# Two copies instead of one of the residual and RMSNorm tiles in an output-projection loop

## The chip, the cores and the metric

One Trainium2 chip, 8 cores, one program on all of them. The time is the device time in microseconds of the slowest core.

## The reference, cut to what matters

The kernel computes one layer of a decoder block for 2 x 8192 tokens of 1024 channels: an attention and a pooling branch, gated and merged, then a channel sub-layer. The part that the change touches is the end of the first sub-layer and the norm in front of the second one:

```
merged = (jax.nn.sigmoid(g_attn) * (attn @ w_branch_attn[l])
          + jax.nn.sigmoid(g_pool) * (pool @ w_branch_pool[l]))
x = x + gate1 * (merged @ w_out[l])

h2 = rms_norm(x, norm2_g[l]) * (1 + scale2) + shift2
u = causal_dwconv(h2 @ w_up[l], conv_w[l], conv_b[l])
```

## The kernel before, in words

Each core owns 2048 tokens, in 16 tiles of 128, and one tile ahead of them (17 tiles in all). The program is a row of stages with a barrier after each: modulation, input projection, attention, output projection (the one that is changed), up-projection with convolution, down-projection. `modrep` in SBUF holds the six modulation vectors, 1024 floats each, in the order shift1, scale1, gate1, shift2, scale2, gate2.

The output-projection stage (lines 802 to 900) goes over five groups of tiles: one of a single tile, then four of four tiles. In each group it first makes the pooling branch tile by tile (lines 843 to 858, PSUM bank 0), then the merged activations `mergedT` in eight pieces (859 to 873, banks 2 to 5, gates loaded from `SGS`), and then runs a loop over the group's tiles (874 to 899). The text gives the steps of that loop letters, with the tile's place in its group behind:

- M: 16 matmuls of `mergedT` with `Wout`, 8 into bank 6 and 8 into bank 7 (lines 877 to 881), on TensorE (PE)
- G: two products with gate1, one for each bank, into the halves of `tmp3` (882), on VectorE (DVE); Ga and Gb are the halves
- A: `x1t = tmp3 + xo` (885), on VectorE; `xo` is the residual input, loaded by line 876, and `x1t` is stored to `X1S` by line 886
- Q: sum of squares of `x1t` into a column of `small3`, the squares themselves into `junk3`, and its root (889, 890), on ScalarE (ACT)
- R: the reciprocal (891); S: `tmp3 = x1t` times it times G2rep (892); H: `h2b = tmp3 + shift2` (893), all on VectorE
- T: eight transposes of `h2b` into bank 0 (894 to 896), on TensorE; C: the copy of bank 0 into `h2T` (897), on ScalarE

`warm(n)` puts in n dummy matmuls of 512 columns into bank 1, whose result nobody reads: 2 per pooling tile, 3 per piece of `mergedT`, 4 after G and 4 after C of each tile. A dummy depends on the operation that stands ahead of it in the program.

The order on each engine's queue isn't that of the program. Within a stage, `schedule` simulates the engines at build time with costs that are written in the kernel, and takes again and again the operation that can start first, out of the next 48 waiting ones of each engine. These lines of it are spoken of below:

```
f += (LAT if (d.eng != e or d.is_dma) else 0.15) + sl
...
if ok and e == 'tensor' and o.mode != pemode[0]:
    ready = max(ready, te + 0.4)
if ok and o.bg:
    ready = max(ready, te) + 0.25
if ok and (best is None or ready < best[0] - 1e-9):
    best = (ready, e, o)
if ok and ready <= te:
    break
```

`te` is the time up to which the engine is taken, `LAT` is 0.35, `bg` marks a dummy, and the `mode` of a transpose differs from that of a matmul. Keys such as `'tmp3'` or `('ps', 0)` (a PSUM bank) carry the dependences; a key with a slot conflicts with the same slot and with the name alone. DMAs that share a semaphore name wait for each other.

Of the kernel before, what the change touches and what calls it, by code (L numbers as in the profile page):

```python
# [7 lines left out]
F32 = mybir.dt.float32  # L8
BF16 = mybir.dt.bfloat16
AF = mybir.ActivationFunctionType  # L10
# [235 lines left out]
def build_nc():  # L246
# [37 lines left out]
    with ExitStack() as st:  # L284
# [29 lines left out]
        def bank(i, n=512, parts=128, off=0):  # L314
            return psum[0:parts, i * 512 + off: i * 512 + off + n]
# [27 lines left out]
        def TR(out, in_, ident, R, W):  # L343
            P.op('tensor', lambda e: e.transpose(out, in_, ident), R, W, dur=(0.42 if in_.dtype == F32 else 0.12),  # L344
                 mode=(rk(in_.shape[0]), rk(fs(in_)), in_.dtype == F32, True))

        def ACT(out, in_, func, R, W, **kw):
            P.op('scalar', lambda e: e.activation(out=out, in_=in_, func=func, **kw), R, W,  # L348
                 dur=edur('scalar', fs(in_)) + (0.1 if 'accum_out' in kw else 0.0))

        def DMA(q, out, in_, R, W, sem):
            nb = fs(out) * out.shape[0] * (4 if out.dtype == F32 else 2)
            P.op(q, lambda e: e.dma_start(out=out, in_=in_), R, W, dma=sem, dur=2.0 + nb / 120000.0)  # L353

        def TT(eng, out, in0, in1, op, R, W):
            P.op(eng, lambda e: e.tensor_tensor(out=out, in0=in0, in1=in1, op=op), R, W, dur=edur(eng, fs(out)))  # L356
# [9 lines left out]
        def STT(out, in0, scalar, in1, op0, op1, R, W):  # L366
            P.op('vector', lambda e: e.scalar_tensor_tensor(out=out, in0=in0, scalar=scalar, in1=in1, op0=op0, op1=op1), R, W,  # L367
                 dur=edur('vector', fs(out)))
# [443 lines left out]
        t1 = T3([512], F32)  # L812
        t2 = T3([512], F32)
        mergedT = T3([8, 512], BF16)
        xo = T3([1024], F32)
        x1t = T3([1024], F32)
        tmp3 = T3([1024], F32)
        h2b = T3([1024], BF16)
        junk3 = T3([1024], BF16)
        small3 = T3([16], F32)  # L820

        CDMA(Wba, wba_d.rearrange("(h d) c -> d h c", d=64), ['Wba'], cast=True)
# [17 lines left out]
        for (tf, ntl) in chunks:  # L840
            N = ntl * 128
            tok0 = tf * 128
            for tl in range(ntl):
                ti = tf + tl
                cb, pb = (0, 4) if ti != 1 else (8, 12)
                for g in range(4):
                    o = bank(0)[:, g * 128:(g + 1) * 128]
                    MM(o, p_own[:, ti, g * 128:(g + 1) * 128], Am[:, cb + g, :], True, ti == 0, ['p_own', 'Am'], [('ps', 0)])
                    if ti >= 1:
                        MM(o, p_own[:, ti - 1, g * 128:(g + 1) * 128], Am[:, pb + g, :], False, True, ['p_own', 'Am'], [('ps', 0)])  # L850
                CP('scalar', pooledT, bank(0).rearrange("p (g t) -> p g t", t=128), [('ps', 0)], ['pooledT'])
                for g in range(4):
                    MM(bank(0)[:, g * 128:(g + 1) * 128], poolw[:, g, :], pooledT[:, g, :], True, True,
                       ['poolw', 'pooledT'], [('ps', 0)])
                for g in range(4):
                    ACT(pool2T[:, g, tl * 128:(tl + 1) * 128], bank(0)[:, g * 128:(g + 1) * 128], AF.Copy,
                        [('ps', 0), 'pscale'], [('pool2T', tl)], scale=pscale[:, g:g + 1])
                warm(2)
            for mt in range(8):
                si = mt % 2  # L860
                DMA('sync', sgc[si][:, 0, 0:N], SGS[mt, :, tok0:tok0 + N], (), [('sgc', si)], 'sgc%d' % si)
                DMA('sync', sgc[si][:, 1, 0:N], SGS[8 + mt, :, tok0:tok0 + N], (), [('sgc', si)], 'sgc%d' % si)
                ba, bp = 2 + (mt % 2), 4 + (mt % 2)
                for hh in range(8):
                    MM(bank(ba, N), Wba[0:64, hh, mt * 128:(mt + 1) * 128], attnT[0:64, hh, tok0:tok0 + N],
                       hh == 0, hh == 7, ['Wba', 'attnT'], [('ps', ba)])
                for g in range(4):
                    MM(bank(bp, N), Wbp[:, g, mt * 128:(mt + 1) * 128], pool2T[:, g, 0:N], g == 0, g == 3,
                       ['Wbp', 'pool2T'], [('ps', bp)])
                TT('vector', t1[:, 0:N], bank(ba, N), sgc[si][:, 0, 0:N], ALU.mult, [('ps', ba), ('sgc', si)], ['t1'])  # L870
                TT('vector', t2[:, 0:N], bank(bp, N), sgc[si][:, 1, 0:N], ALU.mult, [('ps', bp), ('sgc', si)], ['t2'])
                TT('vector', mergedT[:, mt, 0:N], t1[:, 0:N], t2[:, 0:N], ALU.add, ['t1', 't2'], [('mergedT', mt)])
                warm(3)
            for tl in range(ntl):
                ti = tf + tl
                DMA('sync', xo, xw_v[47 + ti], (), ['xo'], 'xo')
                for half in range(2):
                    wb = 6 + half
                    for k in range(8):
                        MM(bank(wb), mergedT[:, k, tl * 128:(tl + 1) * 128], Wout[:, k, half * 512:(half + 1) * 512],  # L880
                           k == 0, k == 7, ['mergedT', 'Wout'], [('ps', wb)])
                    TT('vector', tmp3[:, half * 512:(half + 1) * 512], bank(wb), gate1rep[:, half * 512:(half + 1) * 512],
                       ALU.mult, [('ps', wb), ('modrep', 2)], [('tmp3', half)])
                warm(4)
                TT('vector', x1t, tmp3, xo, ALU.add, ['tmp3', 'xo'], ['x1t'])
                DMA('sync', X1S[ti], x1t, ['x1t'], [('X1S', ti)], 'x1s')
                sm = small3[:, (ti % 4) * 4:(ti % 4) * 4 + 4]
                smk = ('small3', ti % 4)
                ACT(junk3, x1t, AF.Square, ['x1t'], ['junk3', smk], accum_out=sm[:, 0:1])
                ACT(sm[:, 1:2], sm[:, 0:1], AF.Sqrt, [smk], [smk], scale=1.0 / 1024.0, bias=epsb)  # L890
                RECIP(sm[:, 2:3], sm[:, 1:2], [smk], [smk])
                STT(tmp3, x1t, sm[:, 2:3], G2rep, ALU.mult, ALU.mult, ['x1t', smk, 'G2rep'], ['tmp3'])
                TT('vector', h2b, tmp3, shift2rep, ALU.add, ['tmp3', ('modrep', 3)], ['h2b'])
                for k in range(8):
                    TR(bank16(0)[:, k * 128:(k + 1) * 128], h2b[:, k * 128:(k + 1) * 128], ident_bf,
                       ['h2b', 'ident_bf'], [('ps', 0)])
                CP('scalar', h2T[:, :, ti * 128:(ti + 1) * 128], bank16(0).rearrange("p (k t) -> p k t", t=128),
                   [('ps', 0)], [('h2T', ti)])
                warm(4)
# [170 lines left out]
```

How the kernel before makes its waits and increments, by code:

```python
            def body(e):  # L198
# [9 lines left out]
                        if k not in need or need[k][1] < d.val:  # L208
                            need[k] = (d.sem, d.val)
                    if o.force is not None:
                        d = o.force
                        k = id(d.sem)
                        if k not in need or need[k][1] < d.val:
                            need[k] = (d.sem, d.val)
                    for k, (sem, val) in need.items():
                        if wt.get(k, 0) >= val:
                            continue
                        e.wait_ge(sem, val)
                        wt[k] = val
                    ins = o.fn(e)
                    if o.is_dma:
                        ins.then_inc(o.sem, 16)
                    elif o.flag:
                        ins.then_inc(o.sem, 1)
                if eng_name in ('sync', 'gpsimd') or final:
                    for sem, val in dma_final:
                        k = id(sem)
                        if wt.get(k, 0) >= val:
                            continue
                        e.wait_ge(sem, val)
                        wt[k] = val
```

## Time and profile before

| | us |
|---|---|
| median of 2 runs | 3096.95 (3095.92 to 3097.97) |
| the profiled execution | 3089.25 |
| span of its slowest core (core 5) | 3087.7 |
| spans of its eight cores | 3065.0 to 3087.7 |
| output-projection stage on core 5 | from 2136.6 to 2554.5 |

The span runs from the first to the last instruction of the core that was profiled. Times in rows are microseconds from the start of that span unless they are marked ns. Helpers issue all operations, so the lines in rows are those of helpers: L340 a matmul, L344 a transpose, L348 and L372 ScalarE's activations and copies, L353 a DMA, L356 a VectorE operation on two tensors, L367 the one with a scalar column (S), L380 the reciprocal.

### The profile page before, as it was taken

The page shows a single profiled execution, that of the slowest core. Times are in us where ns is not written, and L with a number is a line of the kernel's source. Part 1 is how long each engine was busy: PE and PEld are TensorE (multiplying, and loading weights), DVE is VectorE, ACT ScalarE, POOL GpSimd, SP SyncE. Part 2 cuts the span into 40 slices and gives each one's busy share as a digit, 9 for nine tenths or more (in the row PEclk, how much of TensorE's full clock was granted, in tenths as well). Part 3 has the DMA queues.
Part 4 walks back from the last instruction along what each step waited for, and adds up shares of the span by engine and source line. Part 5 has one row for each costly group of instructions (what it writes and reads, how often), then busy time and mean ns, then how long its engine had stood idle before and what let it go on. Part 6 is the DMA issues. An engine that isn't in the chain of part 4 may idle for free. (4 is left out here: it accounts for less than half of the span.)

```text
span 3087.7 us, 43503 instructions; the slowest of 8 cores (3065.0 to 3087.7 us)
## 1 busy us (share of the span) xinstructions
PE 2446.0 (79%) x15542; PEld 1361.1 (44%) x15542; DVE 1145.2 (37%) x1507; ACT 1659.6 (54%) x2148; POOL 55.7 (2%) x63
## 2 busy tenths in 40 slices
PE   6668888996587878788787878786777778999499
PEld 2234434442455555465555545554333333444144
DVE  0257663221323232322323232321244445888322
ACT  0157775543486868687686868685122115777300
POOL 0000000000000000000000000000000001111000
PEclk9789999998798989899898989898689888999799
DMA  8774442213301010100001000003222213333532
GB/s 264 196 166 136 137 125 82 76 56 104 84 1 32 1 32 1 32 1 19 14 1 32 1 18 1 1 1 56 54 72 80 82 64 41 38 39 37 93 102 103
DMA packets 132450, 191.29 MB, mean 62 GB/s; under 512 B 57168, under 2 KB 102608, under 8 KB 128336
## 3 DMA queue, kind: packets, MB, share of 16 engines
q1 hardware_dynamic: 76192, 158.48, 16.7%
q0 software_dynamic: 56048, 30.02, 7.9%
q8 instruction: 130, 2.13, 0.3%
q14 instruction: 80, 0.66, 0.1%
HBM read 173.24 MB, written 45.22 MB: 71 GB/s over the span
## 5 line engine op out<-in xcount | busy, mean ns | idle before, releaser
L340 PE MATMUL psum<-arena 128*128 128x512 bf16 (+8 forms) x14434 | 2356.8, 313 | 454.8 <-ACT arena L348 116.5
L340 PEld LDWEIGHTS psum<-arena 128*128 128x128 bf16 (+3 forms) x14434 | 1288.4, 102 | 1505.8 <-issue 919.8
L348 ACT ACTIVATE arena<-psum 128x1024 bf16<-128x1024 f32 (+3 forms) x1113 | 999.6, 911 | 407.7 <-PE psum L340 373.1
L356 DVE TENSOR_TENSOR arena<-psum,arena 128x256 f32<-128x256 f32 (+4 forms) x535 | 276.6, 527 | 1238.5 <-PE psum L340 1130.5
L348 ACT ACTIVATE arena<-arena 128x1024 bf16<-128x1024 f32 (+4 forms) x383 | 336.5, 889 | 326.3 <-DVE arena L356 221.2
L367 DVE SCALAR_TENSOR_TENSOR arena<-arena 128x2048 f32<-128x2048 f32 (+3 forms) x195 | 331.7, 1701 | 91.3 <-ACT arena L348 78.4
L356 DVE TENSOR_TENSOR arena<-arena 128x1024 bf16<-128x1024 f32 (+5 forms) x208 | 236.9, 1139 | 70.4 <-PE psum L344 46.1
L372 ACT COPY arena<-psum 128x512 f32<-128x512 f32 (+1 forms) x258 | 185.0, 719 | 137.2 <-PE psum L344 67.6
L344 PE MATMUL psum<-arena 128*128 128x128 bf16 (+1 forms) x1108 | 89.2, 234 | 180.5 <-DVE arena L356 141.8
L380 DVE RECIPROCAL arena<-arena 128x1 f32<-128x1 f32 (+3 forms) x234 | 146.4, 633 | 124.1 <-ACT arena L348 116.4
L344 PEld LDWEIGHTS psum<-arena 128*128 128x128 bf16 (+1 forms) x1108 | 72.7, 111 | 213.9 <-issue 213.9
L372 ACT CAST arena<-psum 128x512 bf16<-128x512 f32 x98 | 57.1, 583 | 105.3 <-PE psum L340 105.3
L523 DVE TENSOR_REDUCE arena<-arena 128x8 f32<-128x512 f32 x81 | 55.4, 684 | 156.1 <-ACT arena L348 156.0
L348 ACT ACTIVATE arena<-psum,arena 128x512 bf16<-128x512 bf16 (+2 forms) x193 | 89.7, 474 | 39.6 <-PE psum L340 26.5
L348 ACT ACT_TABLE_LOAD x19 | 24.4, 1283 | 157.4 <-DMA arena<-xw 80.4
L356 DVE TENSOR_TENSOR arena<-arena,psum 64x256 bf16<-64x256 f32 (+2 forms) x73 | 28.9, 395 | 91.6 <-PE psum L340 91.3
L377 DVE MEMSET arena<- 128x1632 bf16 (+3 forms) x11 | 11.5, 1048 | 137.3 <-PE psum L340 97.2
L353 POOL DMA_DIRECT2D arena<-wup x44 | 38.5, 875 | 680.5 <-POOLq L234 415.0
L374 DVE COPY arena<-psum 128x256 f32<-128x256 f32 (+2 forms) x96 | 42.2, 439 | 22.9 <-PE psum L344 15.9
L353 POOL DMA_DIRECT2D arena<-wba x1 | 0.7, 685 | 1371.7 <-POOLq L234 1371.7
L377 POOL MEMSET arena<- 128x4096 bf16 (+1 forms) x3 | 7.2, 2409 | 611.4 <-POOLq L234 611.1
L686 DVE TENSOR_REDUCE arena<-arena 128x17 f32<-128x544 f32 x24 | 17.2, 717 | 1.8
(18 smaller groups left out, 45.9 us busy)
## 6 DMA issues: line engine op xcount, KB each, us to landing
arena<-xw SPq DMA_DIRECT2D x81, 512.0 KB, 4.3
arena<-ada_w SPq DMA_DIRECT2D x16, 1536.0 KB, 8.2
arena<-wup POOLq DMA_DIRECT2D x44, 256.0 KB, 4.6
X1S<-arena SPq DMA_DIRECT2D x17, 512.0 KB, 2.9
VS<-arena SPq DMA_DIRECT2D x16, 512.0 KB, 3.5
KS<-arena SPq DMA_DIRECT2D x16, 512.0 KB, 3.5
SGS<-arena SPq DMA_DIRECT2D x8, 1024.0 KB, 4.5
arena<-KS SPq DMA_DIRECT2D x8, 1024.0 KB, 8.4
```

The source lines that it names most:

```text
L340: P.op('tensor', lambda e: e.matmul(out, lhsT=lhsT, rhs=rhs, start=start, stop=stop), R, W, dur=d, mode=(rk(lhsT.shape[0]), rk(fs(lhsT)), ...
L344: P.op('tensor', lambda e: e.transpose(out, in_, ident), R, W, dur=(0.42 if in_.dtype == F32 else 0.12), mode=(rk(in_.shape[0]), rk(fs(in_ ...
L348: P.op('scalar', lambda e: e.activation(out=out, in_=in_, func=func, **kw), R, W, dur=edur('scalar', fs(in_)) + (0.1 if 'accum_out' in kw ...
L353: P.op(q, lambda e: e.dma_start(out=out, in_=in_), R, W, dma=sem, dur=2.0 + nb / 120000.0)
L356: P.op(eng, lambda e: e.tensor_tensor(out=out, in0=in0, in1=in1, op=op), R, W, dur=edur(eng, fs(out)))
L367: P.op('vector', lambda e: e.scalar_tensor_tensor(out=out, in0=in0, scalar=scalar, in1=in1, op0=op0, op1=op1), R, W, dur=edur('vector', fs ...
L372: P.op('scalar', lambda e: e.copy(out, in_), R, W, dur=edur(eng, fs(out)))
L374: P.op(eng, lambda e: e.tensor_copy(out, in_), R, W, dur=edur(eng, fs(out)))
L377: P.op(eng, lambda e: e.memset(ap, val), (), W, dur=edur(eng, fs(ap)))
L380: P.op('vector', lambda e: e.reciprocal(out, in_), R, W, dur=0.08 + 8 * fs(out) / 900.0)
L523: P.op('vector', lambda e: e.tensor_reduce(out=sm, in_=sq.rearrange("p (h d) -> p h d", d=64), axis=AX.X, op=ALU.add), ['sq'], [smk])
L686: P.op('vector', lambda e: e.tensor_reduce(out=m, in_=src, axis=AX.X, op=ALU.max), SCK, ['gm'], dur=0.15 + nt * 32 / 900.0)
```

## The change

The five tiles `xo`, `x1t`, `tmp3`, `h2b` and `junk3` become lists of two; the tile number's parity picks one. The second copies lie in memory that is free by then: shift1, scale1 and scale2 in `modrep`, and G1rep behind it (elements 12288 onward of the bf16 view). The keys get the index as a slot or as part of the name, and the two DMAs get two semaphores each. PSUM banks, the dummies, `small3` and the order in which the program lists the operations stay.

```diff
-        xo = T3([1024], F32)
-        x1t = T3([1024], F32)
-        tmp3 = T3([1024], F32)
-        h2b = T3([1024], BF16)
-        junk3 = T3([1024], BF16)
+        xo = [T3([1024], F32), modrep[:, 4096:5120]]
+        x1t = [T3([1024], F32), modrep[:, 0:1024]]
+        tmp3 = [T3([1024], F32), modrep[:, 1024:2048]]
+        h2b = [T3([1024], BF16), a16[:, 12288:12288 + 1024]]
+        junk3 = [T3([1024], BF16), a16[:, 12288 + 1024:12288 + 2048]]
...
-                DMA('sync', xo, xw_v[47 + ti], (), ['xo'], 'xo')
+                bi = ti % 2
+                DMA('sync', xo[bi], xw_v[47 + ti], (), [('xo', bi)], 'xo%d' % bi)
...
-                    TT('vector', tmp3[:, half * 512:(half + 1) * 512], bank(wb), gate1rep[:, half * 512:(half + 1) * 512],
-                       ALU.mult, [('ps', wb), ('modrep', 2)], [('tmp3', half)])
+                    TT('vector', tmp3[bi][:, half * 512:(half + 1) * 512], bank(wb), gate1rep[:, half * 512:(half + 1) * 512],
+                       ALU.mult, [('ps', wb), ('modrep', 2)], [('tmp3_%d' % bi, half)])
                 warm(4)
-                TT('vector', x1t, tmp3, xo, ALU.add, ['tmp3', 'xo'], ['x1t'])
-                DMA('sync', X1S[ti], x1t, ['x1t'], [('X1S', ti)], 'x1s')
+                TT('vector', x1t[bi], tmp3[bi], xo[bi], ALU.add, ['tmp3_%d' % bi, ('xo', bi)], [('x1t', bi)])
+                DMA('sync', X1S[ti], x1t[bi], [('x1t', bi)], [('X1S', ti)], 'x1s%d' % bi)
...
-                ACT(junk3, x1t, AF.Square, ['x1t'], ['junk3', smk], accum_out=sm[:, 0:1])
+                ACT(junk3[bi], x1t[bi], AF.Square, [('x1t', bi)], [('junk3', bi), smk], accum_out=sm[:, 0:1])
...
-                STT(tmp3, x1t, sm[:, 2:3], G2rep, ALU.mult, ALU.mult, ['x1t', smk, 'G2rep'], ['tmp3'])
-                TT('vector', h2b, tmp3, shift2rep, ALU.add, ['tmp3', ('modrep', 3)], ['h2b'])
+                STT(tmp3[bi], x1t[bi], sm[:, 2:3], G2rep, ALU.mult, ALU.mult, [('x1t', bi), smk, 'G2rep'], ['tmp3_%d' % bi])
+                TT('vector', h2b[bi], tmp3[bi], shift2rep, ALU.add, ['tmp3_%d' % bi, ('modrep', 3)], [('h2b', bi)])
                 for k in range(8):
-                    TR(bank16(0)[:, k * 128:(k + 1) * 128], h2b[:, k * 128:(k + 1) * 128], ident_bf,
-                       ['h2b', 'ident_bf'], [('ps', 0)])
+                    TR(bank16(0)[:, k * 128:(k + 1) * 128], h2b[bi][:, k * 128:(k + 1) * 128], ident_bf,
+                       [('h2b', bi), 'ident_bf'], [('ps', 0)])
```

## Rows read from the trace of the kernel before

**Rows 1.** Busy time by engine, clock, DMA share: the stage, then its four tile loops

```profile
2136.60:2554.50 417.90, 296.79 (x1378) 123.10 (x1378) 159.37 (x222) 77.97 (x154) 2.87 (x4) 0.83 0.27 76
2253.36:2290.84 37.48, 27.36 (x127) 11.40 (x128) 20.75 (x25) 9.82 (x16) 0.00 (x0) 0.91 0.36 123
2338.00:2376.70 38.70, 27.01 (x128) 11.25 (x127) 21.80 (x26) 9.82 (x16) 0.00 (x0) 0.91 0.35 120
2424.90:2465.20 40.30, 28.76 (x127) 11.71 (x127) 20.78 (x25) 9.82 (x16) 0.00 (x0) 0.88 0.34 114
2513.50:2553.13 39.63, 30.34 (x128) 12.19 (x129) 20.81 (x25) 9.82 (x16) 0.00 (x0) 0.84 0.27 93
```

**Rows 2.** Timeline of VectorE in the first four-tile loop: start, duration, operation, [idle before]

```profile
2258.62 1.29 DVE L356 TENSOR_TENSOR arena<-psum,arena 128x512 f32<-128x512 f32 x2 [5.26 <-PE psum L340]
2260.16 1.23 DVE L356 TENSOR_TENSOR arena<-arena 128x1024 f32<-128x1024 f32 x1 [0.24 <-DVE arena L356]
2263.11 0.16 DVE L380 RECIPROCAL arena<-arena 128x1 f32<-128x1 f32 x1 [1.73 <-ACT arena L348]
2263.39 1.29 DVE L367 SCALAR_TENSOR_TENSOR arena<-arena 128x1024 f32<-128x1024 f32 x1
2264.78 1.23 DVE L356 TENSOR_TENSOR arena<-arena 128x1024 bf16<-128x1024 f32 x1
2266.11 1.29 DVE L356 TENSOR_TENSOR arena<-psum,arena 128x512 f32<-128x512 f32 x2
2267.64 1.23 DVE L356 TENSOR_TENSOR arena<-arena 128x1024 f32<-128x1024 f32 x1 [0.24 <-DVE arena L356]
...
2287.40 1.23 DVE L356 TENSOR_TENSOR arena<-arena 128x1024 bf16<-128x1024 f32 x1 [0.17 <-DVE arena L367]
```

**Rows 3.** Timeline of ScalarE, same loop: root of Q1, then C1 and C4

```profile
2262.72 0.29 ACT L348 ACTIVATE arena<-arena 128x1 f32<-128x1 f32 x1
2266.96 1.01 ACT L372 COPY arena<-psum 128x1024 bf16<-128x1024 bf16 x1 [3.95 <-PE psum L344]
...
2289.58 1.01 ACT L372 COPY arena<-psum 128x1024 bf16<-128x1024 bf16 x1 [4.00 <-PE psum L344]
```

**Rows 4.** Timeline of TensorE: the first loop, a slow transpose ahead of it, slow projection matmuls

```profile
2194.88 1.01 PE L344 MATMUL psum<-arena 128*128 128x128 bf16 x8 [5.11 <-DVE arena L356]
...
2259.46 4.86 PE L340 MATMUL psum<-arena 128*128 128x512 bf16 x21 [0.30 <-DVE arena L356]
2266.26 0.61 PE L344 MATMUL psum<-arena 128*128 128x128 bf16 x8 [1.94 <-DVE arena L356]
2267.05 6.39 PE L340 MATMUL psum<-arena 128*128 128x512 bf16 x21 [0.18 <-PE psum L344]
...
2288.88 0.61 PE L344 MATMUL psum<-arena 128*128 128x128 bf16 x8 [3.17 <-DVE arena L356]
2290.84 2.79 PE L340 MATMUL psum<-arena 128*128 128x128 bf16 x15 [1.35 <-ACT arena L372]
...
2513.71 6.52 PE L340 MATMUL psum<-arena 128*128 128x512 bf16 x16 [1.27 <-DVE arena L356]
```

**Rows 5.** Timeline of VectorE: first G of the other loops, one H that waits

```profile
2344.19 1.29 DVE L356 TENSOR_TENSOR arena<-psum,arena 128x512 f32<-128x512 f32 x2 [5.04 <-PE psum L340]
...
2431.43 1.29 DVE L356 TENSOR_TENSOR arena<-psum,arena 128x512 f32<-128x512 f32 x2 [6.51 <-PE psum L340]
...
2454.26 1.23 DVE L356 TENSOR_TENSOR arena<-arena 128x1024 bf16<-128x1024 f32 x1 [1.59 <-PE psum L344]
...
2520.12 1.29 DVE L356 TENSOR_TENSOR arena<-psum,arena 128x512 f32<-128x512 f32 x2 [6.56 <-PE psum L340]
```

**Rows 6.** Loads of xw (KB, us to landing); a wait and the busy times near the stage's start

```profile
arena<-xw SPq DMA_DIRECT2D x81, 512.0 KB, 4.3
...
2168.77 1.01 PE L340 MATMUL psum<-arena 128*128 128x512 bf16 x2 [3.29 <-DMA arena<-wout]
...
2140.00:2186.00 46.00, 20.09 (x136) 11.56 (x137) 6.53 (x24) 3.34 (x6) 0.05 (x1) 0.62 0.70 125
```

## The prediction

> **What bounds the kernel now.** I began with the span in equal stretches. The output-projection stage is 417.9 us of the 3087.7 us span, and in it no engine is full: TensorE is busy for 296.8 us, VectorE for 159.4 us, ScalarE for 78.0 us, and the DMA engines have a share of 0.27 [rows 1]. So the stage runs on waits, and averages say nothing about what the change is worth. The change touches only the tile loop at the end of each group of four tiles. I cut that loop out of the timeline for each group, from the first gate product G1 to the first matmul behind the last copy C4 (in the last group, to the dummies that close the stage): 2258.62 to 2290.84 is 32.2 us, 2344.19 to 2376.70 is 32.5, 2431.43 to 2465.20 is 33.8 and 2520.12 to 2553.13 is 33.0 [rows 2, 5]; the ends are those of the windows, set at that matmul [rows 1]. Together 131.5 us, about 4% of the kernel; nothing that happens there can give more than a part of it.
>
> Next, the VectorE timeline of one section [rows 2]. The reader is to see a period: G1 starts at 2258.62 and G2 at 2266.11, 7.5 us later, and the next tiles repeat it. Inside: G 1.29, A 1.23 after a gap of 0.24, then 1.73 us of idling that ScalarE's square and root end, R 0.16, S 1.29, H 1.23. That is 5.2 us of work and some 2.3 us of gaps. G2 can't start before H1 has read `tmp3`, so VectorE has nothing to put into the 1.73 us. A 16-matmul group M2 is meanwhile done early: it starts 0.84 us after G1, and with its five dummies takes 4.86 us [rows 4]. VectorE's one-tile chain bounds the section, then its tail H4, T4, C4: 2287.40 + 1.23 to 2290.84 is 2.2 us [rows 2 to 4]. In the third group H waits 1.59 us for transposes, because there is one `h2b` [rows 5].
>
> **What the change takes away.** No arithmetic is added or removed. With two copies of every tile, G2 need not wait for H1, and the 1.73 us can be filled with G2. The waits for the load of `xo` and the store of `x1t` are relaxed too, which I cost at nothing: the median `xw` load lands 4.3 us after its issue [rows 6], and between the end of A1 (2260.16 + 1.23), which frees the buffer, and A2 at 2267.64 lie 6.3 us [rows 2]; without that cover it would cost up to the 4.3 us per tile.
>
> The Trainium skill, page "Trainium Kernel Development and Optimization", section "Best Practices", advises double-buffering so that DMA and compute overlap. By that alone one would expect the loads to be the gain; the row above says they were covered, and no term of the sum rests on this sentence.
>
> **The new order, from the scheduler.** The queues are written in the order that the kernel's own list scheduler picks, so I walked its rule through the section, with the costs in the code, for the order only. Three of its rules decide. On the PE queue a plain matmul whose inputs are there goes before a dummy (dummies are charged 0.25), and a dummy goes before a transpose (a change of mode is charged 0.4). Among ready operations the earliest wins, ties by program order. Once banks 6 and 7 are freed early, M3 and M4 are always ready before, or within the 0.4 of, T1. So I get, on PE: M1 M2 M3 M4 with two or three dummies in between, then about 12 dummies, the last four of which wait for G4, and only then T1, T2, about 8 dummies, T3, T4. On VectorE: G1 A1 G2a R1 G2b S1 A2 H1 G3 R2 A3 S2 H2 R3 G4a S3 G4b A4 R4 S4 H3 H4. H3 lands behind S4 since it rewrites the `h2b` that T1 reads. On ScalarE: the four squares and roots, then C1 C2 C3 C4. In the kernel before, C1 ran at 2266.96 between the squares of tiles 1 and 2 [rows 3]; transposes and copies, which were spread over the section, now gather at its end. All share bank 0, so they can't overlap each other.
>
> **The sum for one section**, zero at the start of G1, with 0.11 us between VectorE instructions. G1 and A1 end at 2.76. G2a needs 14 of M2's 16 matmuls (the halves alternate), each 4.86/21 = 0.231 us: 0.84 + 14 x 0.231 + 0.1 = 4.2. Then 0.69 for G2a (half of a pair, a little over 1.29/2), R1 to 5.2, G2b to 6.0, S1 to 7.4, A2 to 8.7, H1 to 10.0, G3 to 11.4, R2, A3 to 13.0, S2 to 14.4, H2 to 15.8, R3, G4a to 16.8, S3 to 18.2, G4b to 19.0, A4 to 20.5. R4 waits 1.73 again, to 22.2, S4 ends at 23.8, H3 at 25.1, H4 at 26.5 [rows 2, 4]. In the kernel before, H4 ended 30.0 us after G1. VectorE alone thus gains 3.5 us a section.
>
> The tail takes most of this back. PE's last four dummies start at 19.3. With the clock at its upper level (transposes 0.61 us for eight, dummies 0.23 each), T1 ends at 20.8, ScalarE is through Q4 1.62 us after A4 (2261.39 to 2263.01, that is A1's end to the end of the root), at 22.1, C1 takes 1.01 to 23.2, T2 starts 0.25 later (C4's end at 2290.59 to the matmul at 2290.84) and ends at 24.1, C2, 0.09 behind it, ends at 25.2, the 8 dummies at 26.3, T3 at 27.0, C3 at 28.1, T4 at 29.0, C4 at 30.1, and the next matmul starts at 30.35 [rows 2 to 4]. At the lower level, where eight transposes took 1.01 us and sixteen projection matmuls 6.52, 0.41 each [rows 4], the dummies take 3.3 us and the same steps end at 32.7. The trace before does not show which it would be: behind the 1.94 us gap ahead of T1 matmuls got slower (M3 and its dummies took 6.39 us where the same 21 took 4.86 as M2), while T4, after a wait of 3.17 us, took the short 0.61 [rows 4]. Neither is nearer, so I take the middle, 31.5. Four sections: 126.0 against 131.5, a gain of 5.5 us; the ends are 121.4 (a gain of 10.1) and 130.8 (a gain of 0.7).
>
> The page "PSUM — Partial Sum Buffer", section "Engine vs sequencer instructions", of the Trainium skill says that the queues of ScalarE and VectorE are strictly first in, first out. It is why C1 stands behind Q4; the ScalarE rows agree as far as they go, and the sum used only the rows.
>
> **What is added.** Tile 1's `xo` has its own buffer, so its 512 KB are now asked for at the stage's start, where PE waits 3.29 us for `wout` while data moves at 125 GB/s [rows 6]. If it pushes all of these back it costs 0.52 MB / 125 GB/s = 4.2 us; if it falls into slack, nothing, and a gain has no reason. TensorE is busy 20.1 of those 46 us, so part of the stretch waits for something, but only 3.29 us of it for that weight; I take 1.0, near the lower end. In the SP queue the load stands ahead of the second `SGS` loads, which wait for the first ones anyway. What waits behind T1 on PE, the out-projection, has gone before it; behind C1 on ScalarE stand only copies. The first tile, alone in its group, keeps its order.
>
> Sum: -5.5 + 1.0 = -4.5 us against the profiled execution (3089.25, of which 3087.7 is the span; the four sections are 131.5 of it). The two runs shown have a median of 3096.95, 7.7 us over the profiled one, so I set the same difference against it: 3092.5, given as 3092.
>
> **Rivals.** (1) VectorE stays the bound and the transposes find room earlier, for instance if T1 and T2 come before the dummies. Then a section ends at H4 26.5 + 2.2 = 28.7, four give 114.8, a gain of 16.7 less 1.0: 3081. For it: idle PE time in the section. Against: the scheduler's charges above.
>
> (2) Slower. TensorE's clock falls in the sections, since PE now has waits ahead of M3, M4 and the last dummies. The section then takes its 32.7, and one of M2 to M4 at the lower level delays its G by 14 x (0.41 - 0.231) = 2.5 us: 35.2 a section, 140.8 for four, 9.3 more than before, with the load 10.3: 3107. For it: M3's row in the kernel before, 6.39 us for the same 21 matmuls that took 4.86 as M2 [rows 4]. Against: dummies fill the gaps, and the sections' granted clock was 0.84 to 0.91 [rows 1]. It decides from the point at which that mean falls below about 0.75.
>
> The Trainium skill's page "TensorE: Matmul & The Clock Gate", section "A second HAM failure mode: psum-queue depth-cycling", describes just that, short idles between matmul groups that cycle banks making the clock swing; no row here shows it caused by bank cycling.
>
> (3) The change does nothing that can be seen: G2 is early but the tail eats all, or G2 keeps waiting for another shared thing (banks, `small3`). 3097.
>
> **How the numbers follow.** The forecast has 0.55, rival 1 0.18, rival 2 0.15, rival 3 0.12. The forecast's bounds with the load's bounds run from 3087 (10.1 gained) to 3100 (0.7 gained, 4.2 lost). The range takes in most of rivals 1 and 2 and their neighbours: 3080 to 3105. A measurement of this kernel can tell about 2% (62 us) from no change. To be 2% faster, the four sections would have to lose half of their 131.5 us, where VectorE's own work is already 4 x 20.8 = 83 us; to be 2% slower, each would have to grow by 15 us, more than the 64 projection matmuls add at the lower level (64 x 0.18 = 11.5). I give 0.02 to faster, 0.02 to slower, 0.96 to the same.
>
> **What would show it.** In the changed kernel: on VectorE the 1.73 us wait ahead of R stays whole only for tile 4, and behind A1 some 1.4 us of it stands ahead of G2a; A4 ends near 20.5 after G1; H3 and H4 stand together near 25; T1 comes after the last matmuls and a long row of dummies; four copies C1 to C4 stand in a row at the end of each section, each behind its transposes; a section lasts 30 to 33 us. I am wrong if T1 comes between M2 and M4, if a section lasts under 29 us, if its granted clock is under 0.75, or if the first section's start moves by more than 4 us.

## The result, and the profile after

| | before | after |
|---|---|---|
| median of the runs that are compared, us | 3096.95 | about 3081 |
| profiled execution (span of its slowest core), us | 3089.25 (3087.7) | 3079.12 (3077.6) |
| ratio of the times, 95% interval | | 0.9946 (0.993 to 0.9962) |
| output-projection stage, mean of 8 cores (lowest to highest), us | 418.1 (411.1 to 426.0) | 406.6 (400.6 to 408.0) |

The ratio is a gain of 0.0054 x 3096.95 = 16.7 us (12 to 22), where 4.5 us had been forecast. Runs in which one half of the chip ran at a lower clock stand outside the ratio. The stage accounts for 11.5 us of it in the profiled executions; the up-projection (336.6 and 336.9 us) and the down-projection (193.3 and 194.5) behind it did not shorten. What the timed runs have beyond that may lie in the longest stage of any core, which went from 426.0 to 408.0; that is argued, not shown.

First, the busy times of the changed kernel in the stage and its four loops, on its slowest core (core 7), with the columns of [rows 1].

```profile
2138.41:2545.95 407.54, 290.41 (x1378) 121.37 (x1378) 156.04 (x222) 77.11 (x154) 2.87 (x4) 0.84 0.28 78
2259.57:2297.57 38.00, 27.69 (x121) 11.39 (x122) 19.93 (x24) 9.61 (x16) 0.00 (x0) 0.84 0.38 121
2342.91:2379.60 36.69, 26.74 (x121) 11.15 (x122) 19.93 (x25) 9.61 (x16) 0.00 (x0) 0.86 0.40 126
2425.62:2461.79 36.17, 26.22 (x121) 11.01 (x122) 19.92 (x25) 9.61 (x16) 0.00 (x0) 0.86 0.39 128
2507.16:2543.62 36.46, 27.02 (x125) 11.48 (x126) 19.93 (x24) 9.61 (x16) 0.00 (x0) 0.86 0.24 87
```

The four windows went from 37.5, 38.7, 40.3 and 39.6 us [rows 1] to 38.0, 36.7, 36.2 and 36.5. The M matmuls ahead of G1 are in them, as before.

Then VectorE in the first loop, beside [rows 2].

```profile
2265.75 1.29 DVE L356 TENSOR_TENSOR arena<-psum,arena 128x512 f32<-128x512 f32 x2 [6.18 <-PE psum L340]
2267.21 1.23 DVE L356 TENSOR_TENSOR arena<-arena 128x1024 f32<-128x1024 f32 x1 [0.17 <-DVE arena L356]
2270.04 0.69 DVE L356 TENSOR_TENSOR arena<-psum,arena 128x512 f32<-128x512 f32 x1 [1.60 <-PE psum L340]
2270.65 0.15 DVE L380 RECIPROCAL arena<-arena 128x1 f32<-128x1 f32 x1
...
2283.44 2.36 DVE L356 TENSOR_TENSOR arena<-arena 128x1024 f32<-128x1024 f32 x2 [0.24 <-DVE arena L356]
2287.10 0.16 DVE L380 RECIPROCAL arena<-arena 128x1 f32<-128x1 f32 x1 [1.30 <-ACT arena L348]
2287.37 1.28 DVE L367 SCALAR_TENSOR_TENSOR arena<-arena 128x1024 f32<-128x1024 f32 x1
2288.83 1.23 DVE L356 TENSOR_TENSOR arena<-arena 128x1024 bf16<-128x1024 f32 x1 [0.17 <-DVE arena L367]
```

G2a stands between A1 and R1, and waits 1.60 us for M2's first bank; R1 no longer waits. The row of two at 2283.44 is A4 and H3. Only R4 still waits for ScalarE. H4 ends at 2290.06, 24.3 us after G1 (30.0 before).

TensorE and ScalarE in the same loop, beside [rows 4] and [rows 3].

```profile
2266.59 3.99 PE L340 MATMUL psum<-arena 128*128 128x512 bf16 x17 [0.30 <-DVE arena L356]
2270.88 4.06 PE L340 MATMUL psum<-arena 128*128 128x512 bf16 x18 [0.30 <-DVE arena L380]
2276.16 4.04 PE L340 MATMUL psum<-arena 128*128 128x512 bf16 x18 [1.23 <-DVE arena L356]
2280.36 0.61 PE L344 MATMUL psum<-arena 128*128 128x128 bf16 x8
2286.95 1.01 PE L344 MATMUL psum<-arena 128*128 128x128 bf16 x8 [5.99 <-ACT arena L372]
2288.11 5.60 PE L340 MATMUL psum<-arena 128*128 128x512 bf16 x16
2293.86 0.61 PE L344 MATMUL psum<-arena 128*128 128x128 bf16 x8
2295.72 0.61 PE L344 MATMUL psum<-arena 128*128 128x128 bf16 x8 [1.25 <-ACT arena L372]
...
2297.57 1.04 PE L340 MATMUL psum<-arena 128*128 128x128 bf16 x10 [0.51 <-ACT arena L372]
```

```profile
2284.76 1.06 ACT L348 ACTIVATE arena<-arena 128x1024 bf16<-128x1024 f32 x1 [5.05 <-DVE arena L356]
2285.72 0.19 ACT L348 ACTIVATION_READ_ACCUMULATOR arena<-arena 128x1 f32 x1
2285.81 0.99 ACT L372 COPY arena<-psum 128x1024 bf16<-128x1024 bf16 x1
...
2288.05 1.01 ACT L372 COPY arena<-psum 128x1024 bf16<-128x1024 bf16 x1 [1.05 <-PE psum L344]
2294.56 1.01 ACT L372 COPY arena<-psum 128x1024 bf16<-128x1024 bf16 x1 [5.50 <-PE psum L344]
2296.41 1.01 ACT L372 COPY arena<-psum 128x1024 bf16<-128x1024 bf16 x1 [0.84 <-PE psum L344]
```

The reader sees M2, M3 and M4 in a row with five dummies, then T1 and the tail: T1 is done at 2280.97, but its copy C1 stands in ScalarE's queue behind the square of tile 4 and starts at 2285.81, so T2 waits 5.99 us; 16 dummies of 5.60 us follow, and T3, whose `h2b` was ready at 2285.80, starts only at 2293.86. From G1 to the next matmul are 31.8 us (32.2 in [rows 2, 4]).

To see where the rest came from I cut the whole stage of every core into the same four parts per group: *pool* (from the last copy of the group before to the last cast of a pooled tile), *merge* (to the last sum that makes `mergedT`), *M* (to G1), *loop* (to the end of C4). The first group has one tile. Means of eight cores, us:

```
             one tile               group 2              group 3              group 4              group 5
before  6.3 41.1  4.1  9.7   18.1 34.6  5.4 32.1  17.1 32.1  5.4 32.5  17.3 32.5  5.9 32.7  17.2 32.6  6.1 32.8
after   6.3 43.5  4.1  9.7   21.5 35.3  5.7 31.4  14.8 30.8  5.3 31.1  14.8 32.0  5.1 31.0  14.8 30.8  5.2 31.0
```

Added up over groups 2 to 5: loop -5.5, M -1.4, merge -3.0, pool -3.8, and +2.4 in the one tile's merge part: -11.3 of the stage's -11.5. In groups 3 to 5 alone the pool parts lost 7.2 us. The busy times show how. In the kernel before (core 5), first the pool part of group 2, then pool and merge of group 3:

```profile
2197.00:2220.19 23.19, 20.36 (x78) 8.34 (x78) 0.69 (x1) 6.75 (x16) 0.00 (x0) 0.50 0.00 0
...
2290.59:2307.10 16.51, 12.64 (x78) 5.83 (x78) 0.69 (x1) 6.75 (x17) 0.00 (x0) 0.90 0.00 1
2307.10:2339.16 32.06, 25.04 (x99) 9.29 (x99) 15.48 (x23) 1.47 (x4) 0.00 (x0) 0.89 0.19 54
```

and in the changed kernel (core 7):

```profile
2297.43:2312.17 14.74, 10.64 (x76) 5.06 (x76) 0.69 (x1) 6.75 (x16) 0.00 (x0) 1.00 0.00 0
2312.17:2342.91 30.74, 24.52 (x107) 9.30 (x107) 15.48 (x23) 1.47 (x5) 0.00 (x0) 1.00 0.20 57
```

The pool part runs 76 instead of 78 matmuls in 10.64 us instead of 12.64; the granted clock is 1.00 instead of 0.90, and merge runs 107 matmuls, eight more, in less time. A pool part of the old order has two more values. One is 23.2 us, with the clock at its lower level (0.50, 1.2 of 2.4 GHz) from end to end. Of the 24 pool parts of groups 3 to 5 (8 cores) three were near that (22.8 to 23.2 us) before and none after; of the 8 of group 2 it was two before and six after. The other is 15.5 us, in three of the 24, with the clock near its upper level; here on core 7, group 3:

```profile
2285.84:2301.32 15.48, 11.35 (x78) 5.24 (x78) 0.69 (x1) 6.75 (x16) 0.00 (x0) 0.98 0.00 1
```

So at nearly the same clock the new order is worth 0.7 us a pool part (15.5 to 14.8). By that estimate the order has some 2 of the 7.2 us, and the clock the other 5; it was 1.00 in all 24 of these parts after the change.

### The profile page after: what moved, and what is told of

Its sections match the earlier page's. It is cut to its first block and busy times, and to the rows that moved or that the text cites. A ratio compares the mean times of both kernels' runs of the same rounds, so it can differ in the third digit from the quotient of the medians.

```text
span 3077.6 us, 43493 instructions; the slowest of 8 cores (3062.9 to 3077.6 us)
## 1 busy us (share of the span) xinstructions
PE 2440.0 (79%) x15542; PEld 1359.5 (44%) x15542; DVE 1142.1 (37%) x1507; ACT 1657.8 (54%) x2148; POOL 55.7 (2%) x63
## 5 line engine op out<-in xcount | busy, mean ns | idle before, releaser
L340 PE MATMUL psum<-arena 128*128 128x512 bf16 (+9 forms) x14434 | 2349.3, 313 | 447.3 <-ACT arena L348 111.4
L348 ACT ACTIVATE arena<-psum 128x1024 bf16<-128x1024 f32 (+3 forms) x1113 | 998.9, 911 | 411.1 <-PE psum L340 376.7
L348 ACT ACTIVATE arena<-psum,arena 128x512 bf16<-128x512 bf16 (+2 forms) x193 | 89.7, 474 | 40.3 <-PE psum L340 27.2
L377 DVE MEMSET arena<- 128x1632 bf16 (+3 forms) x11 | 11.5, 1048 | 137.5 <-PE psum L340 97.1
L374 DVE COPY arena<-psum 128x256 f32<-128x256 f32 (+2 forms) x96 | 42.2, 439 | 22.9 <-PE psum L344 15.9
```

Of the source, the lines that this page charges most:

```text
L340: P.op('tensor', lambda e: e.matmul(out, lhsT=lhsT, rhs=rhs, start=start, stop=stop), R, W, dur=d, mode=(rk(lhsT.shape[0]), rk(fs(lhsT)), ...
L374: P.op(eng, lambda e: e.tensor_copy(out, in_), R, W, dur=edur(eng, fs(out)))
L377: P.op(eng, lambda e: e.memset(ap, val), (), W, dur=edur(eng, fs(ap)))
```

## The experiments

Ratios are to the kernel before, from timed runs on the same chip; stage and parts are means of eight cores of one profiled execution. The two profiled stages of the changed kernel are 406.6 and 407.4, but the cores of one execution differ by up to 15 us (411.1 to 426.0 before), so a stage of a single profile says less than the ratio.

**The changed kernel again.** No edit.

> The changed kernel itself, once more, as the yardstick for the others on the same chip. On the cores of its first profile the stage took 406.6 us on average (before: 418.1), made up of four tile loops of 31.0 to 31.4 us (before 32.1 to 32.8), pooling parts of groups 3 to 5 of 14.8 us (before mostly 16.5), their merge parts of 30.8 to 32.0 (before 32.1 to 32.6), a merge part of the lone first tile of 43.5 us (before 41.1), and a pooling part of the second group of 16.4 us on two cores and 23.2 us on six (before 16.4 on six, 23.2 on two). All theories expect the same again within 2 us per part, and a ratio to the kernel before of 0.993 to 0.997.

Ratio 0.9938 (0.9917 to 0.9959), stage 407.4, loops 31.5, 31.1, 30.9 and 31.0, pool 23.2 in group 2 and 14.8 behind it (clock 1.00 in all 24). The pattern repeats; 23.2 in group 2 now on all eight cores.

**The buffers without the new order.** Two copies and all semaphores as changed, but each engine's queue in the order of the kernel before, since the scheduler goes by the old dependences (`sdeps` are those of single tiles):

```diff
...
-                    for d in o.deps:
+                    for d in o.sdeps:
...
```

> The changed kernel with all its second buffers, keys and semaphores, but every engine's queue in the order of the kernel before (the scheduler is shown the old single-buffer dependences). Theory A, the gain comes from the new order of the queues, which the buffers only permit: tile loops stay near 32.2 us each, losing at most the one wait of H3 for transposes, the pooling parts stay at 16.5 and the merge parts at 32, the lone tile's merge part stays at 41; stage 416 to 419 us, ratio 0.998 to 1.001. Theory B, the buffers themselves take away waits at run time: tile loops of about 31 us and a stage near 411 us, ratio 0.998 or less. Theory C, a denser tile loop keeps TensorE's clock up for the parts behind it: since the loop is as before, no gain here either, ratio 1.

Ratio 1.0007 (0.998 to 1.0034), stage 421.5, loops 127.4 together (130.1 before), pool 21.5, 16.2, 18.6 and 18.1, merge 131.8. The buffers alone take 2.7 us off the loops and nothing off the kernel. What pays is the order that the scheduler makes of them. Of the 24 pool parts of groups 3 to 5 the nine at a clock of 0.99 or 1.00 took 15.5 us again, five at 0.50 took 23.2.

**The order behind the loop without the buffers.** The kernel before, with twelve dummies instead of four behind the last copy of a group:

```diff
-                warm(4)
+                warm(12 if tl == 3 else 4)
```

> The kernel before, with single buffers, and eight more dummy matmuls after the last tile of each group of four. The scheduler then puts these dummies into the gaps of the next group's pooling part, and the branch matmuls, which it had put there, come behind the third and fourth pooling tile, nearly as in the changed kernel. Theory A: pooling parts of groups 3 to 5 fall from 16.5 to about 14.8 us and their merge parts from 32 to about 31, 8 us in all, tile loops unchanged at 32 to 33, 2 us more at the stage's end; stage about 412 us, ratio 0.997 to 0.999. Theory C, the shorter parts come from a steadier clock behind denser tile loops: parts stay at 16.5 and 32, the eight dummies cost 2 us more at the end; stage near 420, ratio 1.000 to 1.001.

Ratio 0.9972 (0.9953 to 0.9991): about half of the gain with single tiles. Loops 129.6, pool 15.5, 15.9 and 15.7 in groups 3 to 5, merge 31.2, 30.7 and 31.8. Group 5's pool and merge on its slowest core (core 5):

```profile
2463.11:2478.64 15.53, 12.37 (x78) 5.51 (x78) 0.69 (x1) 6.77 (x17) 0.00 (x0) 0.89 0.00 1
2478.64:2509.30 30.66, 24.52 (x107) 9.30 (x107) 15.48 (x23) 1.48 (x4) 0.00 (x0) 0.99 0.18 52
```

The merge part has the 107 matmuls and nearly the time (30.66 us) of the changed kernel: behind the loop the eight dummies bring the changed kernel's order, but for the place of two dummies. The merge parts of groups 3 to 5 take 93.7 us together, 93.6 in the changed kernel and 97.2 before.

**No dummies in the loop.** The changed kernel without its two `warm(4)` lines in the tile loop:

```diff
                     TT('vector', tmp3[bi][:, half * 512:(half + 1) * 512], ...
-                warm(4)
...
                    [('ps', 0)], [('h2T', ti)])
-                warm(4)
```

> The changed kernel without the eight dummies per tile in the tile loop (136 of 204 in the stage). T1 then goes ahead of M4 and T2 to T4 follow without dummies between them, and the next group's branch matmuls move back into the gaps of its pooling part, as in the kernel before. Theory A, order decides: loops of 27 to 29 us in place of 31, pooling parts back at 16.5 and merge parts back at 32, stage about 405, ratio 0.993 to 0.996. Theory C, the dummies keep TensorE's clock up: without them the clock falls to its lower level, pooling parts take the 23.2 us that were seen at that level and loops 33 or more, stage over 425, ratio over 1.002.

Ratio 0.9977 (0.9937 to 1.0018), stage 415.9. The loops fall to 27.2, 26.8, 26.8 and 27.3, 16.4 us less than in the changed kernel, and every pool part of every core is 22.3 us. The slowest core (core 5), loop, pool and merge:

```profile
2265.80:2293.03 27.23, 14.76 (x84) 6.64 (x82) 19.92 (x24) 9.73 (x16) 0.00 (x0) 0.86 0.46 155
2293.03:2315.37 22.34, 18.68 (x74) 7.91 (x74) 0.69 (x1) 6.77 (x16) 0.00 (x0) 0.50 0.00 0
2315.37:2347.67 32.30, 25.21 (x100) 9.31 (x99) 15.47 (x23) 1.48 (x4) 0.00 (x0) 0.87 0.19 53
```

74 matmuls take 18.68 us at 0.50, where the changed kernel's 76 take 10.64 at 1.00. The place of the branch matmuls isn't the reason: they stand in the pooling's gaps as in the kernel before, and there, with 16 dummies ahead of T4, 21 of the 24 pool parts of groups 3 to 5 ran at 0.88 or more. So it is the dummies left out here (136 of the stage's 290; the 204 above is a miscount) that had kept the clock up, as far as this run shows. The loops came as theory A has them, the pool parts as theory C. The page "TensorE: Matmul & The Clock Gate", section "HAM oscillation — how this bites in real kernels", of the Trainium skill says that a TensorE that waits for DMA between bursts drops to the lower clock, and advises a loop that keeps it busy; this run agrees as to the clock, with 0.50 for 1.00, though its waits are for ScalarE and VectorE.

**Fewer dummies between T2 and T4.** In the changed kernel's TensorE queue, of the 16 dummies between T2 and T3 four stay, six go behind T3 and six behind T4 (`w` are the dummies, `t` the transposes):

```diff
...
+            w, t = pe[i + 1:i + 17], pe[i + 17:i + 33]
+            pe[i + 1:i + 33] = w[:4] + t[:8] + w[4:10] + t[8:] + w[10:]
...
```

> The changed kernel with one thing moved on TensorE's queue and nothing else: of the sixteen dummies that stand between T2 and T3 of a four-tile loop, four stay, T3 follows, then six, T4, and the last six. The order of everything behind the loop stays as it is, which the run with cheaper transposes could not hold. Theory A, the loop's tail is made by those dummies: T3 at about 23.5 us after G1, T4 at 25 to 26, loops of 27 to 28 us in place of 31.1, the last six dummies under the wait for C4; parts behind unchanged (14.8 and 30.8); stage 391 to 396, ratio 0.988 to 0.991. Rival, what the cheaper transposes gained in the loop is necessarily lost behind it, since the dummies have to run somewhere: loops of 28, pooling parts or merge parts 3 us longer, stage 405, ratio 0.994.

Ratio 0.9973 (0.9945 to 1.0002), stage 414.6. The loops are 2 us shorter each (116.3 together); pool 21.5, 18.0, 15.4 and 16.7 and merge 33.8, 33.7, 35.4 and 33.2 take it back and more. The queue behind the moved dummies is the same, and no dummy is added or left out. Pool and merge of group 3 on the slowest core (core 5):

```profile
2283.05:2301.94 18.89, 15.15 (x81) 6.45 (x78) 0.69 (x1) 6.78 (x16) 0.00 (x0) 0.78 0.00 1
2301.94:2336.06 34.12, 28.60 (x108) 10.26 (x107) 15.48 (x23) 1.48 (x4) 0.00 (x0) 0.85 0.18 50
```

108 matmuls in 28.60 us at 0.85, where 107 take 24.52 at 1.00. So it is not only the order behind the loop: the clock there changed when nothing but twelve dummies had moved. Nor is it how close they stand, since eight dummies now stand right ahead of the pooling, and two in the changed kernel. Of the 24 pool parts of groups 3 to 5, nine ran at 0.78 or 0.79 (18.8 to 19.0 us) and fifteen at 1.00 (15.4 us); which stretch of dummies decides isn't shown.

**Two copies of `tmp3` and `h2b` alone.** `xo`, `x1t` and `junk3` single again:

```diff
-                DMA('sync', xo[bi], xw_v[47 + ti], (), [('xo', bi)], 'xo%d' % bi)
+                DMA('sync', xo[0], xw_v[47 + ti], (), [('xo', 0)], 'xo0')
...
-                DMA('sync', X1S[ti], x1t[bi], [('x1t', bi)], [('X1S', ti)], 'x1s%d' % bi)
+                DMA('sync', X1S[ti], x1t[0], [('x1t', 0)], [('X1S', ti)], 'x1s0')
```

> The changed kernel with two copies of tmp3 and h2b only; xo, x1t and junk3 are single as before. Theory A, the loads and stores were covered and what counts is that G need not wait for H: the queue order of the parts behind the loop is the new one, so they keep 14.8 and 31 us; A2 may wait for the single xo (issue half a microsecond after A1, 4.3 us to landing), so loops of 31 to 33 us; stage 406 to 412, ratio 0.994 to 0.997. Rival: the second copies of xo and x1t are what pays, and without them the gain goes: loops of 33 us or more, ratio 0.998 to 1.

Ratio 0.995 (0.9923 to 0.9978), stage 402.4, loops 122.4 (124.6 in the changed kernel). No loss: the loads and stores were covered, as the prediction had it. The Trainium skill's page "Trainium Kernel Development and Optimization", section "Best Practices", advises the second buffer for them; here it gave nothing that can be measured.

**The early load held back.** Tile 1's load of `xo` waits for the first tile's `x1t`:

```diff
-                DMA('sync', xo[bi], xw_v[47 + ti], (), [('xo', bi)], 'xo%d' % bi)
+                DMA('sync', xo[bi], xw_v[47 + ti], [('x1t', 0)] if ti == 1 else (), [('xo', bi)], 'xo%d' % bi)
```

> The changed kernel, but the load of the residual input of tile 1 waits for the sum of tile 0, as in the kernel before, instead of being issued at the stage's start beside the weights. If the early load is what lengthened the lone tile's merge part, that part goes back from 43.5 to about 41 us, and the stage from 406.6 to about 404; if it also set off the long pooling part of the second group (23.2 us on six cores of eight), that part falls to 16.5 on most cores and the stage goes to about 400; ratio 0.991 to 0.995. If the longer first part is scatter, nothing moves: ratio as the changed kernel.

Ratio 0.993 (0.9908 to 0.9952), stage 404.3; the one tile's merge part is 41.5 us (43.5 and 42.4 in the two profiles of the changed kernel, 41.1 before). The early load costs 1 to 2 us there. Group 2's pool stays at 22.3, so the load is not what makes it slow.

**Transposes made cheap to the scheduler.** The charge for a change of mode, 0.4, becomes 0.1 ahead of a transpose:

```diff
-                        ready = max(ready, te + 0.4)
+                        ready = max(ready, te + (0.4 if not o.mode[3] else 0.1))
```

> The changed kernel, but the scheduler charges transposes 0.1 in place of 0.4 for the change of mode, so that they go before the dummies: T1 comes before M4, T2 after it, T3 two dummies later, and eight dummies stand between T3 and T4 in place of sixteen between T2 and T3. Theory A, the tail of the tile loop is made by dummies that stand ahead of T3 on TensorE's queue (5.6 us of them in the changed kernel's first loop, while H3 had been done for 8 us): loops of about 28 us in place of 31.1; the parts behind them, of which the order changes only a little, stay within 1 us; stage about 395 us, ratio 0.990 to 0.992. Rival: the tail is VectorE's own chain up to H4, and the order of the transposes changes nothing: loops of 31 us, ratio as the changed kernel, 0.994.

Ratio 0.9933 (0.9909 to 0.9956), stage 414.1. The loops fall to 110.4 together, 27.6 each: rival 1's section, without its gain. The merge parts of groups 3 to 5 are 39.6, 40.5 and 40.5 us, at a mean clock of 0.79: the scheduler filled them in another order, with the branch matmuls that used to stand in the pooling's gaps. The ratio and the profiled stage don't fit here (20 us against 4); I draw nothing from it but that the loop's gain didn't come through: the ratio is the changed kernel's.

**A second bank for the transposes.** The changed kernel, T of even tiles in bank 4:

```diff
+                tb = 0 if bi else 4
...
-                CP('scalar', h2T[:, :, ti * 128:(ti + 1) * 128], bank16(0).rearrange("p (k t) -> p k t", t=128),
-                   [('ps', 0)], [('h2T', ti)])
+                CP('scalar', h2T[:, :, ti * 128:(ti + 1) * 128], bank16(tb).rearrange("p (k t) -> p k t", t=128),
+                   [('ps', tb)], [('h2T', ti)])
```

> The changed kernel, with the transposes of even tiles in PSUM bank 4, which is idle in the tile loop, in place of bank 0, so that copies and transposes of neighbouring tiles need not wait for each other, and the next group's pooling, which works in bank 0, need not wait for C4. The scheduler then puts most of the next group's pooling ahead of T4. Theory A: the chain through the shared bank 0 costs real time; the pooling parts of groups 3 to 5 (14.8 us each behind the loop) move largely into the loop's tail, stage 380 to 395 us, ratio 0.983 to 0.990. Rival: ScalarE and TensorE then collide (pooling copies ahead of C4), and what is gained in one part is lost in the other: stage 400 to 410, ratio 0.992 to 0.996.

Ratio 0.9918 (0.9889 to 0.9948), stage 397.1. Bank 0 is now free for the next group's pooling before the section ends, so the loops (39.8 us in groups 2 to 4) contain it, and the pool parts are below zero (-1.2 and three times -3.3). The merge parts grow to 41 to 42, since the branch matmuls no longer have the pooling's gaps. In groups 3 to 5 that is no gain: loop and next pooling together fall by 28.3 us against the changed kernel, and merge grows by 31.8. The gain is at the lone first tile, whose loop and group 2's pooling fall from 31.2 to 11.4 us, while merge grows by 5.7.

**Both: second bank and late load.** The edits of the two runs together.

> The changed kernel with the transposes of even tiles in PSUM bank 4, and tile 1's load of xo held back until the first tile's x1t is there. If the two gains add, the stage means 395 to 396 us (397.1 with two banks alone, less the 1 to 2 us that the late load gave), the lone tile's merge part 41 to 41.5 us, and the ratio to the kernel before 0.990 to 0.992. If the late load's gain was chance of the profile, the stage stays at 397 and the merge part at 43.

Ratio 0.9882 (0.9843 to 0.9921), stage 392.2 (389.7 to 396.5): the lowest ratio of all, though its interval overlaps that of the second bank without the late load; 3053.4 us (median of four) against 3088.0 (of six) for the kernel before. The one tile's merge part is 40.5 (43.0 with two banks alone). TensorE at the end of group 3's section, slowest core (core 0):

```profile
2334.49 1.00 PE L344 MATMUL psum<-arena 128*128 128x128 bf16 x15 [0.18 <-DVE arena L380]
2340.69 1.01 PE L344 MATMUL psum<-arena 128*128 128x128 bf16 x8 [5.20 <-ACT arena L372]
2341.85 3.52 PE L340 MATMUL psum<-arena 128*128 128x512 bf16 x16
...
2347.36 1.04 PE L340 MATMUL psum<-arena 128*128 128x128 bf16 x10 [0.47 <-ACT arena L348]
2348.78 1.25 PE L340 MATMUL psum<-arena 128*128 128x128 bf16 x8 [0.39 <-ACT arena L372]
...
2357.35 0.61 PE L344 MATMUL psum<-arena 128*128 128x128 bf16 x8
```

T1 and T2 go together (the row of 15; one of the 16 isn't in the trace), T3 follows, and the pooling (the rows of 10 and 8) runs ahead of T4 at 2357.35, which waits for nothing.

**The second bank alone.** The kernel before, single tiles, T of even tiles in bank 4.

> The kernel before (single tiles), only with the transposes of even tiles in PSUM bank 4. Theory 'order': what pays is that the next group's pooling matmuls find room inside the section once bank 0 is free for them, and no second copy of a tile is needed for that: stage 400 to 408 us, ratio 0.992 to 0.996, parts of loop and next pooling together 45 to 47 us (49.8 before). Theory 'copies': VectorE's one-tile chain still ends the section, so nothing moves: stage 414 to 422, ratio 0.999 to 1.002, loop and next pooling 49 to 50 us.

Ratio 0.9905 (0.9874 to 0.9936), stage 398.4. Loop and next pooling together are 40.1, 41.7 and 40.4 us where they were 49.2, 49.8 and 49.9; merge takes back part of it (41.1, 41.0, 34.7, 41.1). The lone tile's loop and group 2's pooling fall from 27.8 to 11.5 us, and merge grows by 6.4 there: about half of the stage's 19.7 us. The second bank, without any second copy, is worth no less than the whole change (0.9874 to 0.9936 beside 0.993 to 0.9962), and with the bank the copies add nothing that can be told apart (0.9918 and 0.9905).

**Everything for the loop's end.** The moved dummies, the late load, and twelve dummies behind the first tile:

```diff
-                warm(4)
+                warm(12 if ti == 0 else 4)
```

> The run before with two things more: the late load of tile 1's residual input, and eight more dummies behind the lone first tile, so that the second group's pooling part gets the order that groups 3 to 5 have. Theory A: another 1 to 2 us from the load, and the second group's pooling part 14.8 in place of 16.4 where the clock is at its upper level. If the dummies also keep that clock up there, as they do in groups 3 to 5, the 23.2 us that most cores show in that part go too: stage 380 to 384, ratio 0.985 to 0.988. If the clock in that part hangs on something else (the idling ahead of it), it stays near 21 us: stage 388 to 393, ratio 0.988 to 0.990.

Ratio 0.999 (0.9964 to 1.0015), stage 405.9. Group 2's pool is 16.1 at a clock of 0.85 and not 0.50 any more, so dummies behind the first tile mend that place; groups 3 to 5 keep what moving the dummies cost (pool 17.6, 15.4 and 17.9, merge 33.4 to 34.4). Neither theory's time came; the profiled stage, little shorter than the changed kernel's 406.6, and the ratio don't fit here either.

## Why the prediction was wrong

The direction and the loop were right, the size was not: 4.5 us forecast, 16.7 (12 to 22) measured.

**The step that failed** is the frame of the sum: that the change touches only the tile loop, "about 4% of the kernel; nothing that happens there can give more than a part of it", so that the sum needed two terms. The new dependences changed what the scheduler wrote behind the loop as well, and with the dummies' places in the loop the clock of what follows changed. The missing terms measured -3.8 us in the pool parts (-7.2 in groups 3 to 5, +3.4 in group 2), -3.0 in merge and -1.4 in M. I had walked the scheduler's rule through the section and stopped at its end; going on into the pooling and merge operations behind it would have shown the moved dummies and branch matmuls. The clock could be read before: pool at 0.90 and merge at 0.89 in the rows of the kernel before shown above, with 23.2 us where it fell to 0.50. I looked up the clock only for the whole stage, its start and the loops.

**The loop.** Forecast -5.5 for four, measured -5.5 as a mean of cores; the section 31.5, measured 31.8 in the first. Part of that is luck within the tail. VectorE was 2 us faster than I had it: A4 ended 18.9 after G1 (2283.44 + about 1.2 - 2265.75), forecast 20.5, and H4 24.3, forecast 26.5. H3 ran right behind A4, not behind S4, since T1 stood ahead of the dummies and freed its `h2b` early. On the other side, the 12 dummies foretold ahead of T1 and 8 behind T2 came as two ahead of T1 and 16 behind T2: T2 ended 22.2 after G1 (24.1 forecast), the dummies 28.0 (26.3), T3 28.7 (27.0), the next matmul 31.8 (30.35 at the upper clock level, 32.7 at the lower). The tail is what ends the section, as foretold, and its dummies ran between the levels, 5.60/16 = 0.35 us, at a mean granted clock of 0.64.

**The load.** Taken at 1.0 between 0 and 4.2; the one tile's merge part grew by 2.4 (1.3 in the second profile), and holding the load back took 1 to 2 of it away.

**"The first tile keeps its order"** held for the loop. But the first section began 126.1 us after the stage's start, 119.3 before (sums of the parts up to G1): 6.8 later, over the 4 us that I had named as a sign of being wrong. 2.4 of it stands in the one tile's merge part, where the load is, 3.4 in the pool part of group 2, which fell to the lower level on six cores instead of two. Why more often is open. TensorE's queue up to there is the same in nine of the profiled runs: in the three with one `xo` it was 8 of 24 cores, in the six with two 41 of 48. The load at the stage's start isn't it (7 of 8 with that load held back), and more dummies ahead of it prevent it.

**Rivals.** Rival 1's 3081 was the time, not the mechanism: VectorE was not the bound in the section. Two orders that came near its section (27 to 28 us, without loop dummies and with cheap transposes) shortened the loops and gave it back behind them. Rival 2, a falling clock: in the four windows the mean granted clock went from 0.84 to 0.91 [rows 1] down to 0.84 to 0.86, far from the 0.75 that was named, and outside the section it rose; the run without dummies shows the fall where I hadn't looked. Rival 3 is ruled out by the ratio.

What the gain behind the loops is made of is shown in kind, and in shares only for the pool parts. With the old order there is no gain. Dummies behind the last copy bring about half without a second buffer (0.9972, interval 0.9953 to 0.9991). With the new order behind the loop but the 16 dummies spread out, the pool and merge parts of groups 2 to 5 take 207.7 us (194.6 in the changed kernel, 201.5 before), and the ratio can't be told from 1. In the pool parts, old-order parts at 0.98 and new ones at 1.00 set the order's share at about 2 of 7.2 us and the clock's at about 5. For merge that isn't shown, since no merge part of groups 3 to 5 in the old order ran above 0.89, and why the new order keeps the clock at 1.00 isn't shown either. An order with C1 ahead of tile 4's square on ScalarE was not tried.

## What to carry to other kernels

Where an automatic scheduler writes the queues, a second buffer is a new order, and the sum has to go past the loop it is in, up to the point where both orders agree again, with the granted clock of each part beside it. Before taking out filler work or waits, look at what stands behind them: four runs here shortened the loop by 2 to 4 us a section beyond the changed kernel and lost it in the next stretch. And ask which shared thing holds up the tail: one more PSUM bank for the transposes was worth 1% by itself, no less than five doubled tiles. Then look where it pays: with the doubled tiles all of its gain, and without them half, lay behind the lone first tile, while behind the other groups merge took back all or most of what the tail gave.

## What the runs showed of the hardware

The clock was the surprise. Eight transposes behind a wait of 5.99 us took 1.01 us at a granted clock of 0.50, 16 dummies behind them 5.60 (0.35 each) at a mean of 0.64, and the next eight transposes 0.61 at 1.00: within that row of dummies TensorE came back to its upper level. The same pooling in the same order took 15.5 us at a granted clock of 0.98 to 1.00, 16.5 at 0.90, and 23.2 at 0.50, where it stayed from the first to the last matmul. The cores of one execution of the kernel before differed in which of the three they got. Without the loop's dummies all 32 pool parts stayed at 0.50 (22.3 us); in the changed kernel's order the 24 of groups 3 to 5 ran at 1.00 (14.8 us), in both profiles.
